# Head of a two-layer hybrid block: small parameters on another queue, conditioning vectors first, modulation weights cut by rows instead of by columns

## The reference, cut to what matters

```python
def hybrid_layer(x, ctx, c, c_ctx, p, cos, sin, update_ctx):
    mod_x = jax.nn.silu(c) @ p['ada_w'] + p['ada_b']          # (1024) @ (1024, 3072)
    mod_c = jax.nn.silu(c_ctx) @ p['ada_w'] + p['ada_b']
    shift_x, scale_x, gate_x = jnp.split(mod_x[:, None, :], 3, axis=-1)
    shift_c, scale_c, gate_c = jnp.split(mod_c, 3)
    px = in_projection(rmsnorm(x, p['norm_w']) * (1 + scale_x) + shift_x, p['w_in'])
    pc = in_projection(rmsnorm(ctx, p['norm_w']) * (1 + scale_c) + shift_c, p['w_in'])
    # gated linear attention (GLA), gated DeltaNet, latent attention on px and pc,
    # then the three are gated, merged, projected and added:
    x = x + gate_x * merge_branches(...)
```

## Time and profile before

| | |
|---|---|
| median of 3 runs | 2557.88 us (2553.23 to 2560.52) |
| profiled execution | 2558.39 us, span of the core 2556.6 us |
| PE busy | 2249.1 us, 88% of the span |
| DVE, ACT, POOL busy | 957.2 us (37%), 808.4 us (32%), 351.3 us (14%) |
| mean granted clock of PE | 0.935 of full speed |

### The profile page before, as it was taken

How to read it: one execution, slowest core, us unless ns; L and a number is a source line. 1 busy time by engine, 2 the same in 40 slices (tenths; PEclk the granted TensorE clock), 3 DMA queues, 4 the chain that set the end, 5 groups by cost and what they waited for, 6 DMA issues and landing times. The chain is left out here.

```text
span 2556.6 us, 32145 instructions
## 1 busy us (share of the span) xinstructions
PE 2249.1 (88%) x11226; PEld 1511.6 (59%) x11226; DVE 957.2 (37%) x2389; ACT 808.4 (32%) x2165; POOL 351.3 (14%) x568
## 2 busy tenths in 40 slices
PE   6998987798987978999999999988687886889998
PEld 3675555555554666555674447756465564766687
DVE  1023354554554324333331111246555563233321
ACT  2223333333433123444321122334323332235421
POOL 1000005052423000000000000001460532000000
PEclk8999989798988999999999999999797988999999
DMA  8215321121212112111222242113221312223233
GB/s 286 80 33 165 101 71 60 48 62 46 88 37 71 42 58 68 42 50 43 68 66 82 104 148 69 49 34 103 71 74 55 104 53 58 80 68 101 93 122 132
DMA packets 224735, 203.84 MB, mean 80 GB/s; under 512 B 29999, under 2 KB 220035, under 8 KB 224067
## 3 DMA queue, kind: packets, MB, share of 16 engines
q1 hardware_dynamic: 220608, 187.93, 23.9%
q0 software_dynamic: 2400, 13.52, 1.5%
q10 hardware_dynamic: 1571, 0.34, 0.1%
HBM read 184.91 MB, written 16.85 MB: 79 GB/s over the span
## 5 line engine op out<-in xcount | busy, mean ns | idle before, releaser
L1035 PE MATMUL bank<-hT,ring 128*128 128x512 f32 (+2 forms) x1856 | 727.3, 540 | 13.9 <-ACT WORK L1579 8.1
L1035 PEld LDWEIGHTS bank<-hT,ring 128*128 128x128 f32 (+1 forms) x1856 | 338.3, 192 | 280.4 <-issue 245.0
L1035 PE MATMUL bank<-ring,hT 128*128 128x256 f32 (+2 forms) x2112 | 465.2, 376 | 39.2 <-DVE O L1790 19.8
L1035 PEld LDWEIGHTS bank<-ring,hT 128*128 128x128 f32 x2112 | 389.2, 194 | 115.4 <-issue 37.0
L1035 PE MATMUL bank<-WORK 128*128 128x128 f32 (+5 forms) x2160 | 375.0, 324 | 43.0 <-issue 16.3
L1035 PEld LDWEIGHTS bank<-WORK 128*128 128x128 f32 (+2 forms) x2160 | 300.8, 196 | 144.9 <-issue 118.3
L1035 PE MATMUL bank<-yT,ring 128*128 128x512 f32 (+1 forms) x768 | 276.8, 494 | 0.0
L1035 PEld LDWEIGHTS bank<-yT,ring 128*128 128x128 f32 x768 | 139.2, 193 | 80.4 <-issue 71.5
L1004 POOL TENSOR_TENSOR WORK<-WORK 64x31 f32<-64x31 f32 (+15 forms) x248 | 150.3, 606 | 19.4
L1002 POOL TENSOR_TENSOR WORK<-WORK 64x31 f32<-64x31 f32 (+15 forms) x248 | 146.4, 590 | 19.5
L1940 DVE SCALAR_TENSOR_TENSOR WORK<-WORK,CW 128x512 f32<-128x512 f32 (+1 forms) x192 | 145.8, 760 | 3.2
(11 more groups left out here) (195 smaller groups left out, 2219.7 us busy)
## 6 DMA issues: line engine op xcount, KB each, us to landing
ring<-in_w_in_dram SPq DMA_DIRECT2D x92, 1024.0 KB, 5.4
ring<-in_ada_w_dram SPq DMA_DIRECT2D x24, 1024.0 KB, 6.0
ring<-in_w_branch_dram SPq DMA_DIRECT2D x24, 1024.0 KB, 5.0
LD<-WORK SPq DMA_DIRECT2D x64, 128.0 KB, 1.9
ring<-in_w_out_dram SPq DMA_DIRECT2D x8, 1024.0 KB, 5.0
ring<-in_mla_q_up_dram SPq DMA_DIRECT2D x8, 576.0 KB, 4.6
xs<-yT POOLq DMA_DIRECT2D x2, 2048.0 KB, 11.1
O<-XD SPq DMA_DIRECT2D x32, 128.0 KB, 2.5
```

Source lines behind the costliest of these rows:

```text
L1035: return nc.tensor.matmul(o, a, b, start=start, stop=stop, skip_group_check=True)
```

## The change

It has three parts. The 18 loads of parameters move from ACT's queue to POOL's, ahead of the GLA gate's loads. The two loads of `c` and `c_ctx` move to SP's queue, ahead of the token tiles, and have a semaphore of their own. A unit of `ada_w` becomes half of the rows (four tiles of 128) by 512 columns instead of all rows by 256 columns; it has the same 1 MB. A `mod` item then does 8 products of 512 columns instead of 16 of 256, and waits for each of its units only at the first product that reads it. The number of pieces stays four.

```diff
     if k == "mod":
-        return two("ada", it[2])
+        return [(("ada", l, it[2], i), 0, 2 * UNIT) for i in range(2)]
...
-            return {"kup": KVL // P, "qup": QL // P}.get(u[0], KT)
+            return {"kup": KVL // P, "qup": QL // P, "ada": KT // 2}.get(u[0], KT)
...
-            at = {"ada": lambda: (ada_w[l], u[2] * 512 + u[3] * UNIT),
+            at = {"ada": lambda: (ada_w[l][u[3] * D // 2:(u[3] + 1) * D // 2], u[2] * 512),
...
             sp.dma_start(K[:, 0:C_CEN], consts[:, 0:C_CEN]).then_inc(s_const, 16)
+            for row, src in ((PR_C, c[0]), (PR_CC, c_ctx)):
+                sp.dma_start(MT[row:row + 8, 0, 0:P], src.rearrange("(r c) -> r c", c=P)).then_inc(s_cond, 16)
...
             pool.memset(MT[:, 4:7, :], 0.0).then_inc(s_xzset, 1)
+            for row, src in ((PR_NORM, norm_w), (PR_ADAB, ada_b), (PR_GLA, gla_norm_w), (PR_GDN, gdn_norm_w),
+                             (PR_QN, mla_q_norm_w), (PR_KVN, mla_kv_norm_w), (PR_QNN, mla_qn_nope), (PR_KNN, mla_kn_nope)):
+                n = src.shape[1] // P
+                pool.dma_start(MT[row:row + n, 0:DEPTH, 0:P], src.rearrange("l (r c) -> r l c", c=P)).then_inc(s_par, 16)
...
                 elif k == "par":
-                    pe.wait_ge(s_par, 16 * 12)
+                    pe.wait_ge(s_cond, 32)
+                    pe.wait_ge(s_par, 16 * 10)
...
                 elif k == "mod":
-                    units_here(pe, it)
                     pe.wait_ge(*done(("par", 0), "dve"))
-                    todo = [(i, kk) for i in range(2) for kk in range(KT)]
-                    n = len(todo) // (last_piece + 1)
-                    for i, kk in todo[piece * n:piece * n + n]:
-                        grp = kk % NGRP
-                        ins = mm(ps[grp * 32:(grp + 1) * 32, i * UNIT:(i + 1) * UNIT], SCP[:, 2 * kk:2 * kk + 32],
-                                 weights(it, i)[:, kk, :], kk < NGRP, kk >= KT - NGRP)
+                    n = KT // (last_piece + 1)
+                    for kk in range(piece * n, piece * n + n):
+                        grp, half = kk % NGRP, kk // (KT // 2)
+                        u = units_of(it)[half][0]
+                        pe.wait_ge(s_unit[slot[u]], 16 * load_of[u])
+                        ins = mm(ps[grp * 32:(grp + 1) * 32, :], SCP[:, 2 * kk:2 * kk + 32],
+                                 weights(it, half)[:, kk % (KT // 2), :], kk < NGRP, kk >= KT - NGRP)
```

More of the change, by code:

```diff
@@ L616, in hybrid_block @@
         s_tok = [stack.enter_context(nc.semaphore(f"tokens_in{tt}")) for tt in range(TT)]
+        s_cond = stack.enter_context(nc.semaphore("conditioning_in"))
         s_par = stack.enter_context(nc.semaphore("par_in"))
@@ L956, in _ @@
             pool.memset(MT[:, 4:7, :], 0.0).then_inc(s_xzset, 1)
+            for row, src in ((PR_NORM, norm_w), (PR_ADAB, ada_b), (PR_GLA, gla_norm_w), (PR_GDN, gdn_norm_w),
+                             (PR_QN, mla_q_norm_w), (PR_KVN, mla_kv_norm_w), (PR_QNN, mla_qn_nope), (PR_KNN, mla_kn_nope)):
+                n = src.shape[1] // P
+                pool.dma_start(MT[row:row + n, 0:DEPTH, 0:P], src.rearrange("l (r c) -> r l c", c=P)).then_inc(s_par, 16)
+            for l in range(DEPTH):
+                pool.dma_start(MT[0:CONV * 24, 2 + l, 0:P], gdn_conv_w[l].rearrange("j (r c) -> (j r) c", c=P)).then_inc(s_par, 16)
+            for l in range(DEPTH):
+                pool.dma_start(ALB[:, l, 0:16], gdn_a_log[l].rearrange("r h -> (r h)").partition_broadcast(P)).then_inc(s_row, 16)
+                pool.dma_start(ALB[:, l, 16:32], gdn_dt_bias[l].rearrange("r h -> (r h)").partition_broadcast(P)).then_inc(s_row, 16)
+                pool.dma_start(RW[:, l, 0, :], mla_qn_rope[l].partition_broadcast(P)).then_inc(s_row, 16)
+                pool.dma_start(RW[:, l, 1, :], mla_kn_rope[l].partition_broadcast(P)).then_inc(s_row, 16)
             for it in plan:
@@ L1406, in row_rstd @@
                 return nc.scalar.activation(mS[:, at:at + n], mS[:, at:at + n], ACT.Exp, scale=-0.5)
[L1408 to L1413, removed]
-            for l in range(DEPTH):
-                act.dma_start(MT[0:CONV * 24, 2 + l, 0:P], gdn_conv_w[l].rearrange("j (r c) -> (j r) c", c=P)).then_inc(s_par, 16)
-            for l in range(DEPTH):
-                act.dma_start(ALB[:, l, 0:16], gdn_a_log[l].rearrange("r h -> (r h)").partition_broadcast(P)).then_inc(s_row, 16)
-                act.dma_start(ALB[:, l, 16:32], gdn_dt_bias[l].rearrange("r h -> (r h)").partition_broadcast(P)).then_inc(s_row, 16)
-                act.dma_start(RW[:, l, 0, :], mla_qn_rope[l].partition_broadcast(P)).then_inc(s_row, 16)
-                act.dma_start(RW[:, l, 1, :], mla_kn_rope[l].partition_broadcast(P)).then_inc(s_row, 16)
             nc.scalar.preload_act_table_set("natural_log_exp_and_others")
```

## The result

| | before | changed |
|---|---|---|
| median of 12 runs each, one chip | 2555.79 us (2550.95 to 2561.36) | 2562.94 us (2557.37 to 2566.78) |
| profiled execution | 2558.39 us, span 2556.6 | 2566.78 us, span 2565.0 |
| mean granted clock of PE | 0.935 | 0.931 |

The ratio is 1.0026, 95% interval 1.0015 to 1.0037: slower by 6.6 us (0.0026 x 2556), which is within the 0.3% taken as no change. The forecast was 2560.6, with a range of 2554 to 2568. The time came out inside the range, 2.3 us above the forecast. Part of that nearness is luck: the forecast was built on the 2557.9 of three runs, and twelve runs put the kernel before at 2555.8. Taken as a change, the forecast was 2.7 us slower and the measured one is 6.6. One of the two large terms of the sum had not happened.

The account below looks back on a forecast made before the run. The prediction took the head as bound by the second unit's load, then by a PE, ACT and DVE chain, and the GLA stretch by PE. 2558.4 - 5.5 + 8.0 + 0.2 = 2561.1, median 2560.6, range 2554 to 2568.

Parts of the forecast that it names:

- Pieces, 8.0 us lost: GLA branch's second half: 24 two-strip pieces cost 0.41 us more each, 18 paid, plus 0.6 for half clock; 8.0 us lost.
- The idle times that were to hide six pieces: GLA branch's second half: PE waits of 3.69, 0.84 (twice) and 1.27 us absorb six pieces' extra time.
- The half-clock piece: Piece at 211.01 us, after idle time, runs at about half the clock; its extra is 0.8 us, not 0.4.
- ACT off the path, second unit on it: Head: the second unit's landing at 22.8 us, not ACT, ends the wait; freeing ACT alone leaves `mod` starting at 23.
- I take this stall as gone: Head: SP's 10.99 us issue stall vanishes, second unit lands at 19.1 us, first `mod` ends 5.8 us earlier.
- the gate's rows taken as the price of POOL's loads: Head: POOL's parameter loads cost what gate loads do, 0.51 us to issue and 5.5 us to land.
- The tenth added to a unit's 2.8 us: Head: allowance for other queues sharing the engines, so the second unit lands 3.1 us after the first.
- The dear end's reading: Head: POOL issues at 1 us each and loads land in 19.0 us, putting `SCP` at 33; first `mod` 10 us late.
- It follows the end of the first `mod` at the distance it has now: Head: `lr` keeps its distance behind the first `mod` if loads come in time; head gains 5.5 us.
- The rival of the slowest engines: Head: POOL's small packets hold up the slowest DMA engine, second unit lands at 23.7 or later; 2566.3 us, chance 0.20.
- All hidden: Rival: pieces cost 1 us or less and the head gains all, 2550.4 us or a little below; chance 0.08.
- Third rival, 2561.4: Head gains only 1.2 us, pieces at their low end of 4.2 us lost; 2561.4 us, chance 0.10.

Follow-up runs that it names:

- e1: Kernel before with only units cut by rows and products of 512 columns, all small loads still on ACT's queue; ratio to before 1.0005.
- e3: Changed kernel with each 512 columns done as two times 256, so a piece fills four strips; full sum over rows left out; ratio to before 1.0006.
- e4: Changed kernel with a woven `mod` cut into two pieces of four 512-column products instead of four pieces; ratio to before 0.9998.
- e2: Kernel before with only the small loads moved to POOL's and SP's queues, units and products as before; ratio to before 1.0001.
- e6: e5 with conditioning vectors first on SP, ACT's table load first, then `par`'s parameters on ACT, broadcasts on ACT at the first `mod`; ratio to before 0.9990.
- e5: e1 with woven pieces of 256 columns over half the rows, filling four strips; whole `mod` items as eight products of 512; ratio to before 0.9991.
- e8: e1 with only the eight loads that copy a row to 128 partitions (`ALB`, `RW`) moved to POOL's queue; ratio to before 1.0028.
- e7: Changed kernel with the eight broadcast loads (`ALB`, `RW`) on ACT's queue behind its table load; ratio to before 1.0020.
- e9: e5 with 28 unused products added in the head where PE would stand idle; ratio to before 0.9984.

## Why the prediction was right, and where it was wrong

The time was in the range because the larger term, the pieces, was sized well, and a failed gain of the head was small enough for the range. The head was to gain 5.5 us and lost 0.8, and the first product after the last piece came 8.4 us later, where some 2.5 was the sign named. That the time is only 2.3 us from the likeliest is in part luck, since the kernel before measured 2.1 us less in twelve runs than in three.

- **Pieces, 8.0 us lost: right, by its own reasons.** Measured 7.5 in the changed kernel, 7.35 in `e1`. The step came out at 0.98, and `e3` and `e4` show that it was the empty strips. The idle times that were to hide six pieces shrank by 0.42, 0.84 (twice) and 0.42. The half-clock piece is there too (1.72 at 225.99), though at another place than before.
- **ACT off the path, second unit on it: right.** In `e2` ACT is free early and the second unit still ends the wait (7.29 us); `lr` did not move forward. In `e6` the second unit lands at 17.3, and there the first `mod` starts 3.5 us earlier than in `e5` with ACT's work ahead. So ACT mattered once the units were early.
- **"I take this stall as gone": right of SP, wrong of the unit.** SP's issue did not stall, and the first four units were queued by 9.24 us. The first unit landed at 13.7, earlier than the 16.0 of the sum, and the second still at 20.8 and not at 19.1. The step that failed is the one before it, the gate's rows taken as the price of POOL's loads. It holds for the time to issue (0.53 to 0.75 us each) and for the ten loads of `par`, whose last one was issued at 7.55 and landed at 13.2. It doesn't hold for the broadcasts, nor does it say what they take from others: their packets of 512 B lasted 576 ns in the mean, on engines that the units need. The tenth added to a unit's 2.8 us "since other queues share the engines" was that term, mis-sized: the second unit came 20.8 - 13.7 = 7.1 us after the first, not 3.1. With no broadcasts on POOL's queue it came 2.7 to 4.4 us after it in `e6`, `e5` and `e1`. The dear end's reading, `SCP` at 33 and so 7 us past what it now holds up, is off by itself: 33 is 10 us past 23.02.
- **"It follows the end of the first `mod` at the distance it has now": wrong.** The 3.8 us that were gained at 22.83 were gone at 37.16. The third and fourth units came late by the same traffic. The prediction kept PE's rates as they were, but PE stood idle once more ahead of the second `mod`'s last half (1.22 us) and went through the norm's stretches behind both waits at the lower clock. `e5` against `e1` prices such a fall of the clock at up to 3.6 us of `lr`. In `e4`, with the same head, about half of the loss did not happen, so its size differs by execution.
- **The rival of the slowest engines** had a chance of 0.20 and forecast 2566.3, 8.4 us over the median that it began from; measured were 6.6, as a change nearer to it than to the forecast's 2.7. Of its mechanism, `e8` shows that small packets from POOL hold up the units; that the slowest engine ends each of them is not shown. Its trigger was put wrongly: it was to act by a first `mod` that ends no earlier than 26.4. The rule it leaned on, that the queues share 16 engines and another queue saves only issue time (the Trainium skill, DMA: Bandwidth & Descriptors, "Issuing engines are not separate DMA queues"), agrees with the trace in that POOL's and SP's packets run side by side (39.4% and 63.7% of the engines' time from 10 to 20 us). What decided here was another quantity, the engines' time for the same broadcasts: 14.9 us from ACT's queue before, over 60 from POOL's in the changed kernel (40.3 for the packets of 512 B, and 34.6 - 11.2 = 23.4 for the further ones of 2 KB, if the others took what they took in `e7`).
- **All hidden, 0.08:** fell, no product started early in the empty strips. **Third rival, 2561.4:** its time was near, its piece term of 4.2 was not.

Left open: why a broadcast's packet is long from POOL's queue while others of that queue are not, and why either half of them costs 4 us of `lr` against `e7`. Open too is how much of the second unit's delay in the changed kernel the broadcasts made, since `e7` delayed its first units in another way. The records don't name the engine a packet ran on, so whether one slow engine ends each unit could not be seen. It was not tried to send the broadcasts from POOL after the head, behind `lr`.

## What to carry to other kernels

Cutting a weight by rows instead of columns kept the bytes and doubled the DMA row, and gave this head 1.9 to 5.5 us, by the clock of the execution. But it changed how many products a woven piece has, so count the strips that each piece fills, not only the whole item. Moving small loads off a busy engine to POOL's queue gained nothing here, since a weight load ended the wait; see first what ends it, and then what the loads do on the new queue to the big ones. And when a stage waits on transfers, price what follows each wait at both clock levels.

## What the runs showed of the hardware

- A load that copies one row to 128 partitions: from ACT's queue 512 packets of 64 B at 11 ns and 512 of 256 B at 18 ns; from POOL's 64 to 70 packets of 512 B at 418 to 841 ns in the mean, single ones up to 2.2 us (`e3`). Eight such loads on POOL's queue made the first four units land 2.5 to 6.1 us later (`e8` against `e1` and `e5`) and the kernel 5.9 us slower by the ratios, give or take 4 (`e8` against `e1`).
- The granted clock in the head stood at 0.50 or 1.00 for the same program up to there (`e5`, `e1`). With 28 products without a use, in time when PE had nothing to do, it was at 1.00 in the one execution profiled (`e9`).
- Row length: units with rows of 2 KB moved 394 GB/s at a DMA share of 1.04 (25 to 27.5 us of the changed kernel), those with rows of 1 KB 371 at 1.10. In the mean of the first 30 us a packet of 2 KB took 91 ns there and one of 1 KB 52 ns in the kernel before.
